# First three expert blocks of the last pass kept on chip, activations laid out by partition, and four table rows fetched in the first key half

## What is computed

```python
qh = (hb @ w_q).reshape(tb, PEER_HEADS, 2, PEER_HALF)
s1 = jnp.einsum('thd,nd->thn', qh[:, :, 0], keys1)
s2 = jnp.einsum('thd,nd->thn', qh[:, :, 1], keys2)
...
best, pos = lax.top_k(cand, PEER_TOPK)
eidx = jnp.take_along_axis(cidx, pos, axis=-1)
gates = jax.nn.softmax(best.astype(jnp.float32), axis=-1).astype(hb.dtype)
act = jax.nn.gelu(jnp.einsum('td,thkd->thk', hb, u_tab[eidx]), approximate=False)
return jnp.einsum('thk,thkd->td', gates * act, v_tab[eidx])
```

## Time and profile before

| what | value |
|---|---|
| median of 3 runs | 2736.82 us (2735.11 to 2752.26) |
| the profiled execution | 2736.22 us, its span 2734.4 us |
| PE busy | 2642.6 us (97% of the span) |
| DVE busy | 1921.7 us (70%) |
| POOL busy | 1311.6 us (48%) |
| ACT busy | 1067.2 us (39%) |
| moved | 539.31 MB, mean 197 GB/s |

### The profile page before, as it was taken

How to read it: one execution, slowest core, us unless ns; L and a number is a source line. 1 busy time by engine, 2 the same in 40 slices (tenths; PEclk the granted TensorE clock), 3 DMA queues, 4 the chain that set the end, 5 groups by cost and what they waited for, 6 DMA issues and landing times. The chain is left out here.

```text
span 2734.4 us, 37662 instructions
## 1 busy us (share of the span) xinstructions
PE 2642.6 (97%) x13717; PEld 2229.8 (82%) x13717; DVE 1921.7 (70%) x3096; ACT 1067.2 (39%) x1703; POOL 1311.6 (48%) x622
## 2 busy tenths in 40 slices
PE   8999999999899999999999999999999799999997
PEld 6888887665788887878777899999999788888885
DVE  5445242787854447599776387768999689888897
ACT  4322321455342323352223233335666544444443
POOL 4444452211444445454124467782323368877883
PEclk9999999999999999999899999999999999999998
DMA  5444342112334444332012265558999999999994
GB/s 194 146 143 145 106 166 62 56 54 74 104 123 154 146 138 153 101 110 67 16 63 87 83 179 163 166 157 338 401 392 389 373 359 386 384 385 387 386 387 168
DMA packets 190912, 539.31 MB, mean 197 GB/s; under 512 B 14416, under 2 KB 96464, under 8 KB 170704
## 3 DMA queue, kind: packets, MB, share of 16 engines
q1 hardware_dynamic: 88688, 306.23, 33.6%
q0 software_dynamic: 18432, 134.23, 12.2%
q10 hardware_dynamic: 83680, 97.46, 10.3%
HBM read 482.28 MB, written 55.57 MB: 197 GB/s over the span
## 5 line engine op out<-in xcount | busy, mean ns | idle before, releaser
L358 POOL TENSOR_TENSOR ring_low<-ring,ring_high 128x1024 fp32r<-128x1024 f32 x323 | 801.3, 2482 | 984.4 <-ACT ring_high L318 979.7
L318 ACT ACTIVATE ring_high<-ring 128x1024 fp32r<-128x1024 f32 x354 | 374.2, 1057 | 617.9 <-PE ps L415 485.4
L413 PE MATMUL ps<-u,ring_high 128*128 128x512 f32 (+1 forms) x1504 | 565.8, 376 | 19.6 <-DVE u L520 10.0
L414 PE MATMUL ps<-u,ring_high 128*128 128x512 f32 (+1 forms) x1504 | 559.9, 372 | 0.0
L415 PE MATMUL ps<-u,ring_low 128*128 128x512 f32 (+1 forms) x1504 | 559.7, 372 | 0.0
L358 POOL TENSOR_TENSOR ring_low_more<-ring,ring_high_more 128x1024 fp32r<-128x1024 f32 x103 | 266.8, 2593 | 153.6 <-ACT ring_high_more L318 152.8
L413 PEld LDWEIGHTS ps<-u,ring_high 128*128 128x128 f32 x1504 | 284.0, 189 | 63.4 <-POOL ring_low L641 10.0
L414 PEld LDWEIGHTS ps<-u,ring_high 128*128 128x128 f32 x1504 | 284.2, 189 | 40.1 <-issue 1.4
L415 PEld LDWEIGHTS ps<-u,ring_low 128*128 128x128 f32 x1504 | 284.0, 189 | 39.3
L2867 POOL DMA_INDIRECT fetched_rows<-in_peer_uv,fetch_index x128 | 157.4, 1230 | 180.1 <-DVE ps L2887 138.1
L3487 DVE TENSOR_TENSOR expert_product<-group_acts,group_weights 128x384 f32<-128x384 f32 x128 | 162.9, 1273 | 70.0 <-issue 50.8
(11 more groups left out here) (476 smaller groups left out, 5269.8 us busy)
## 6 DMA issues: line engine op xcount, KB each, us to landing
ring<-in_peer_u SPq DMA_DIRECT2D x128, 512.0 KB
ring<-in_peer_uv SPq DMA_DIRECT2D x128, 512.0 KB
ring<-in_ffn_gu SPq DMA_DIRECT2D x88, 512.0 KB
ada_weights<-in_ada_w SPq DMA_DIRECT2D x48, 512.0 KB, 3.9
ring<-in_ffn_down SPq DMA_DIRECT2D x48, 512.0 KB
expert_acts<-kept_acts ACTq DMA_DIRECT2D x128, 192.0 KB
expert_weights<-weight_stage ACTq DMA_DIRECT2D x24, 1024.0 KB
group_acts<-expert_acts ACTq DMA_DIRECT2D x15, 1536.0 KB
```

The lines of the kernel that those rows point to most:

```text
L318: act.activation(k.highs[p], k.ring[:, s], ACT.Copy).then_inc(k.high_ready[p].sem, 1)
L358: pool.tensor_tensor(k.lows[p], k.ring[:, s], k.highs[p].bitcast(F32), ALU.subtract)\
L413: pe.matmul(out, k.highs[p][:, w], high, start=first, stop=False)
L414: pe.matmul(out, k.highs[p][:, w], low, start=False, stop=False)
```

## The change

Three things change, all between the first key half and the last pass.

**Activations by partition.** `expert_acts` is stored as [partition, expert block, token] instead of [expert block, partition, token]. A store still consists of 128 pieces of 1536 bytes. A load of eight expert blocks becomes 128 pieces of 12288 bytes instead of 1024 pieces of 1536 bytes.

**Expert blocks 0 to 2 of the last pass.** A class `Edge` owns buffers that don't overlap `weigh`. SP loads the activations of blocks 0 to 2 and their gates for token blocks 0 to 17 ahead of the last four `u` chunks of `weigh` (`midway`), those for token blocks 18 to 21 behind the last ring load of `weigh`; the last two token blocks ACT copies from the two slots. A piece of these gate loads has 192 bytes. DVE makes the first two products and the first remainder within `weigh`, ACT rounds the `v` chunks 1 to 3 there too, and DVE instead of POOL forms their remainders. What is left of group 0 comes in two loads after the last multiply of `weigh`: blocks 3 and 4 (gate pieces of 128 bytes), then blocks 5 to 7 (192 bytes). ACT issues the load of group 1 behind block 3 instead of block 1.

**Four rows early.** The indices of the gathered rows are worked out in the first key half, and POOL issues the first four fetches there, in its last quarter behind chunk 6.

The core of the diff:

```diff
@@ load (of the ring)
+        if midway is not None:
+            midway()
         for j in range(SLOTS, self.n):
@@
-EDGE = 2
+EDGE = 3
+SECOND = 5
+SOONER = 4
+class Edge:
...
+    SOON = NB - 6
...
+    def load_blocks(self, k, sp, lo, hi):
+        for slot in range(2):
+            sp.wait_ge(self.x.staged[slot].sem, 16 * ((hi + 1 - slot) // 2))
+        sp.dma_start(self.weights[:, lo:hi], k.dram["expert_weights"][lo:hi, :, 0:EDGE].rearrange("b p e t -> p b (e t)"))\
+          .then_inc(self.loaded.sem, 16)
+    def load(self, k, sp):
+        for s in range(EDGE):
+            sp.wait_ge(self.x.stored[s].sem, 16)
+        sp.dma_start(self.acts[:], k.dram["expert_acts"][:, 0:EDGE]).then_inc(self.loaded.sem, 16)
+        self.load_blocks(k, sp, 0, self.SOON)
+    def copy(self, act):
+        x = self.x
+        for b in range(2):
+            act.wait_ge(x.taken[b].sem, x.taken[b].at(NB))
+        for slot in range(2):
+            copy = act.activation(self.weights[:, NB - 2 + slot].rearrange("p (e t) -> p e t", t=WT),
+                                  x.stage[:, slot, 0:EDGE], ACT.Copy)
+        copy.then_inc(self.copied.sem, 1)
...
+    def first(self, dve, n):
+        if n == 0:
+            for b in range(2):
+                dve.wait_ge(self.x.weighed[b].sem, NB)
+            dve.wait_ge(self.loaded.sem, 48)
+            dve.wait_ge(self.copied.sem, 1)
...
@@ route, POOL
+                        if j == 6 and i == QT - 1:
+                            pool.wait_ge(indexed.sem, 1)
+                            pool.wait_ge(scored.sem, 4 * QT)
+                            for c in range(SOONER):
+                                x.fetch(k, pool, c)
@@ keep_acts
-        act.dma_start(k.dram["expert_acts"][n], acts[:, n % ACTS]).then_inc(x.stored[n % ACTS].sem, 16)
+        act.dma_start(k.dram["expert_acts"][:, n], acts[:, n % ACTS]).then_inc(x.stored[n % ACTS].sem, 16)
@@ weigh, SP
-            stream.load(sp)
+            stream.load(sp, midway=lambda: edge.load(k, sp))
+            edge.load_blocks(k, sp, edge.SOON, NB - 2)
@@ weigh, ACT
+                if i == U_ITERS - 1 and e == 6:
+                    edge.copy(act)
                 if GB and 1 <= e < 7:
                     x.gate_row(act, i * PER_U + e - 1)
+                if i == U_ITERS - 1 and e >= 5:
+                    stream.split_high(act, U_ITERS, e - 4)
+                if i == U_ITERS - 1 and e == 6:
+                    edge.round(act, 0)
@@ combine, SP
-            load_weights(sp, 0, NB - 1, 0, 8, weights_loaded[0])
-            load_acts(sp, 0, 0, EDGE, first_acts)
-            load_acts(sp, 0, EDGE, 8, acts_loaded[0])
+            load_weights(sp, 0, NB - 1, EDGE, SECOND, second)
+            load_acts(sp, 0, EDGE, SECOND, second)
+            load_weights(sp, 0, NB - 1, SECOND, 8, weights_loaded[0])
+            load_acts(sp, 0, SECOND, 8, acts_loaded[0])
@@ combine, load_acts
-            eng.dma_start(acts[:, g % 2, lo:hi], k.dram["expert_acts"][8 * g + lo:8 * g + hi].rearrange("e p t -> p e t"))\
+            eng.dma_start(acts[:, g % 2, lo:hi], k.dram["expert_acts"][:, 8 * g + lo:8 * g + hi])\
```

132 lines of the change are left out of this document (86 added, 46 removed).

## The result

| what | before | after |
|---|---|---|
| median of 20 runs each | 2735.84 us | 2740.74 us |
| ratio, 95% interval | | 1.0019 (1.0010 to 1.0027) |
| span of the profiled execution | 2734.4 us | 2741.1 us |

By the medians the change makes the kernel 5 us slower, and the interval lies above 1; 12 us faster was forecast. The hole at the handover did shrink and the waits of the tail went, but PE works more slowly through the whole last pass.

What follows compares the result with a forecast made beforehand. PE was taken to set the pace, with the DMA engines full too. The terms -13.8 + 2.2 - 1.1 + 1.0 + 1.0 + 1.2 - 3 = -12.5 gave 2724.3 us, range 2715 to 2737.

Steps and rivals of the forecast that it cites:

- The hole: PE's stall between weigh and the last pass: 1.5 us instead of 15.3, so -13.8 us.
- the first two products on DVE wait for the copies only: Handover step: products need only ACT's two new copies, take 1.03 us and end before the coefficient's rounding at 2172.4.
- The third block: Last pass: PE waits for block 3's product, held by the load of blocks 3 and 4; +2.2 us (1.3 to 5.0).
- rival C: Small gate pieces cost double, 54 ns instead of 12, holding the third block 9.9 us; about 2737 us, chance 0.12.
- The fifth block: Last pass: its v chunk, loaded behind both loads, makes its remainder late; +1.0 us (0 to 2).
- The clock: Behind the handover: half of the 2.2 us lost at the lower clock level comes back; -1.1 us.
- The edge loads: In weigh, ahead of a u chunk: they make that chunk land late; +1.0 us (0 to 2.3).
- Rival D: Edge loads starve in weigh, one q1 piece a turn; costs from 29 us of loads, 2747 to 2771 us, chance 0.10.
- The four fetches: Last key quarter: POOL's fetches make a chunk's remainder late and PE waits; +1.2 us (0 to 2.5).
- The tail: Last groups: larger activation pieces speed the load, half of PE's 6.0 us of waits go; -3 us.
- B: Rival: the larger share of transfers removes all 6.0 us of tail waits; 2721.3 us, chance 0.12.
- A: Rival: transfers stay at their limit and the tail's 6.0 us of waits remain; 2727.3 us, chance 0.24.

Runs made afterwards that it cites:

- coefs_down_64: Changed kernel with the buffers of products, coefficients and edge tiles 64 bytes lower in each partition; 2732.5 us, ratio to before 0.9991.
- before_coefs_up_64: Kernel before with 64 bytes left free in front of the coefficient buffers, nothing else; 2751.17 us, ratio 1.0048.
- second_by_act: On coefs_down_64, the load of blocks 5 to 7 issued by ACT behind its two copies instead of by SP; 2733.12 us, ratio to before 0.9988.
- no_early: On coefs_down_64, without the four early fetches, the indices still worked out early; 2737.94 us, ratio to before 0.9992.
- fetch_at_four: On second_by_act, the four early fetches placed behind chunk 4 instead of chunk 6; 2732.39 us, ratio to before 0.9978.
- fetch_at_end: On second_by_act, the four early fetches moved behind POOL's last remainder of the first key half; 2738.51 us, ratio to before 1.0019.

## Why the prediction was wrong

- **The sum had no term for PE's own pace.** It took 4.07 us a block from the earlier trace rows for the changed kernel too. The change moved the coefficients' buffers, which the prediction named nowhere as an edit, and each of 2304 matmuls became 6.6 ns longer: 15.3 us (1.9 in the handover's 16 blocks, 11.5 in the middle, the rest in the last two groups). This step failed. Two runs show it in both directions: coefs_down_64 takes the 64 bytes out of the changed kernel, before_coefs_up_64 puts them into the one before. In time it makes about half of the miss of 16 us, and it alone put the kernel outside the range and made it slower than before: with it mended the kernel takes 2732.5 us, which its interval (0.9977 to 1.0006) doesn't tell from the kernel before.
- **The hole**, -13.8 expected, -12.4 measured (15.3 to 2.9). The step that failed is "the first two products on DVE wait for the copies only": they waited 3.15 us for the gates of token blocks 18 to 21, issued at 2164.90. SP was through with the four chunks ahead of them at 2163.25, and then waited for the store of token block 21, issued at 2152.17, to land at 2164.83; the load itself took 12.7 us more.
- **The third block**, +2.2 expected, no wait measured. The load took 10.1 us (2176.90 to 2186.98) where 10.4 were forecast, and its pieces of 128 bytes took 13 ns each where 12 were taken, beside full queues, so rival C with its 54 falls; the longer hole (1.4 us) and the first block, which ran in part at the lower clock (5.7 us instead of 4.1), covered it.
- **The fifth block**, +1.0 expected, 4.3 measured; and a wait of 2.3 for the sixth, which the prediction didn't have, behind a remainder held for 7.9 us, in which POOL issues a fetch and runs three remainders. SP's holds at its issues (6.48 us at the first) were in the earlier trace rows with 8.84, and the prediction made nothing of them; second_by_act shows that they made the chunk late.
- **The clock**, -1.1 expected. The 60.1 us behind the hole ran at a mean of 0.94, which is about 3.6 us lost against 2.2 before: +1.4. Three waits of 2.9, 4.3 and 2.3 us replaced one of 15.3, and the lower level (0.50, that is 1.2 GHz) followed the first two: the granted clock was 0.50 from 2179.6 to 2182.0 and 0.70 from 2202.3 to 2208.0, but 1.00 behind the third.
- **The edge loads**, +1.0 expected; `weigh` took 0.2 longer. Without the early rows it takes 2.8 longer (no_early), so with that stage's scatter of 1.7 us the loads cost between nothing and some 3 us. Rival D was wrong: the chunk behind the loads landed 21.4 us after the first of them was issued, where D loses from 29. (The row that the prediction names for a piece of 8 KB gives 0.28 us and not its 0.32; in the changed kernel's trace such a piece took 0.31 to 0.34 in this stretch, so the sum stands.)
- **The four fetches**, +1.2 expected, +2.9 measured, and by another mechanism: not a late chunk (PE waited 0.4 us for one) but the held DVE operation.
- **The tail**, -3 expected, -7.4 measured in the changed kernel, and that after 1.9 us of slower matmuls. B was right there, A wrong: the layout alone brings -6.9 and -9.3 in the last two columns of stages. That is more than the 6.0 us of waits that bounded this term, since the longest of them also cost clock: before ran at 0.85 for the 11.1 us behind its wait of 4.2 us. In the changed kernel the slower PE helped too.
- **The range** ended at 2737 because the only costs in it were late loads.

With the address mended the 2732.5 us are 8 from the forecast, and by the stages the handover's misses make about as much: 80 us instead of the 71 that the terms gave. Of the other terms there, the tail brought -1.7 instead of -3 and the fetches cost 2.9 instead of 1.2, while `weigh` came out 1.9 below its term.

## What to carry to other kernels

When a change moves buffers, read their addresses as part of the change, and compare counts per stretch, not busy shares: an engine at 100% can still have become slower. A stall that is closed may also have been the time in which others got ahead, so ask who used it. Where several queues are full, count the pieces left on the slowest engine, not the bytes.

## What was not expected of the hardware

- The pace of a matmul depends on the stationary operand's address against the moving one's, modulo 256 bytes: 226.7 ns where they agree, 233.3 where they are 64 bytes apart, some 232 to 235 at the steps with 128 bytes of difference. The Trainium skill ("SBUF — State Buffer", Who interferes with whom) gives PE two independent read ports; these runs show a pace that depends on how the two operands' addresses lie to each other. Why is open.
- A two-input DVE operation of 0.29 us was held for 25.8 us beside an unbroken row of nine POOL operations, and took 0.29 us again when it came ahead of the row (fetch_at_four). In before, larger ones got in between two POOL operations of such a row; what decides is open.
- Leaving a stage with four indirect fetches just issued cost 11 us (fetch_at_end).
